# The down projection in seven block products, set between the tiles of gate and up, with weights handled in halves

## What is computed

```python
h2 = rms_norm(x, g_pre_ffn[l]) * (1.0 + sc2) + sh2
gate, up = jnp.split(h2 @ w_ffn_in[l], 2, axis=-1)      # 1024 x 2816 each
y = (jax.nn.silu(gate) * up) @ w_ffn_out[l]             # 2816 -> 1024
x = x + gt2 * rms_norm(y, g_post_ffn[l])
```

## Time and profile before

| | us |
|---|---|
| median of 3 runs | 1180.68 |
| range of the runs | 1180.19 to 1182.68 |
| span of the profiled execution | 1179.1 |
| PE busy in it | 1141.8 |
| DVE busy in it | 743.3 |
| POOL busy in it | 659.9 |
| ACT busy in it | 306.2 |

### The profile page before, as it was taken

The page is one execution under the profiler, slowest core; times in us unless marked ns, Lnnn a source line. Parts: engine busy times, 40 slices in busy tenths (PEclk is TensorE's granted clock), DMA queues, the critical chain, the costliest instruction groups (busy, mean ns, idle before and its releaser), DMA issues.

```text
span 1179.1 us, 13776 instructions
## 1 busy us (share of the span) xinstructions
PE 1141.8 (97%) x5528; PEld 952.8 (81%) x5528; DVE 743.3 (63%) x895; ACT 306.2 (26%) x460; POOL 659.9 (56%) x387
## 2 busy tenths in 40 slices
PE   2999999999999999999999999999999999999997
PEld 2788888888887888878888888888888888888885
DVE  6986979979997655658745454444444444444448
ACT  5645253362441624341110101010101010101014
POOL 4155343344342550325495958686867777777854
PEclk9999999999999999999999999999999999999999
DMA  9554323232211162211112121202020202020216
GB/s 329 175 161 123 108 74 106 73 107 75 87 36 37 39 231 88 89 36 54 36 36 72 36 72 36 72 26 83 20 88 18 89 19 90 19 89 18 89 32 272
DMA packets 94241, 98.52 MB, mean 84 GB/s; under 512 B 2941, under 2 KB 80994, under 8 KB 94178
## 3 DMA queue, kind: packets, MB, share of 16 engines
q1 hardware_dynamic: 92720, 93.33, 25.1%
q10 hardware_dynamic: 1458, 4.31, 0.9%
HBM read 89.25 MB, written 8.39 MB: 83 GB/s over the span
## 4 chain that ended last, share of the span: by engine, by line
PE 91%; DVE 4%; ACT 2%; issue 1%; SPq 1%; DMA 1%; DVEq 0%; ACTq 0%
PE pair L1732 30%; PE pair L1653 25%; PE pair L1545 24%; PE pair L1581 4%; PE pair L1710 1%; PE pair L1508 1%; DMA x<-in_x 1%; DVE sraw L1261 1%; DVE acc L963 1%; PE pair L1595 1%; PE pair L1576 1%; SPq L404 1%; PE pair L1469 1%; PE pair L1457 1%; PE pair L1597 1%
## 5 line engine op out<-in xcount | busy, mean ns | idle before, releaser
L1085 DVE SCALAR_TENSOR_TENSOR pair<-u,conv_w_col,pair 128x512 f32<-128x512 f32 x240 | 162.4, 748 | 1.2
L1397 DVE TENSOR_TENSOR yt<-yt,pair 128x1024 f32<-128x1024 f32 x80 | 97.5, 1219 | 95.0 <-PE pair L1653 95.0
L607 POOL TENSOR_TENSOR w_lo<-raw,w_hi 128x1024 fp32r<-128x1024 f32 x66 | 146.6, 2222 | 5.3
L605 POOL CAST w_hi<-raw 128x1024 fp32r<-128x1024 f32 x66 | 68.6, 1040 | 121.0 <-PE pair L1653 52.5
L528 POOL TENSOR_TENSOR w_lo<-raw,w_hi 128x1024 fp32r<-128x1024 f32 x21 | 52.4, 2500 | 103.3 <-ACT w_hi L693 103.3
L1653 PE MATMUL pair<-w_hi,u_hi 128*128 128x512 f32 x352 | 108.6, 390 | 0.3 <-DVE yt L1395 0.3
L1653 PE MATMUL pair<-w_hi,u_lo 128*128 128x512 f32 x352 | 108.4, 389 | 0.0
L1653 PE MATMUL pair<-w_lo,u_hi 128*128 128x512 f32 x352 | 108.4, 389 | 0.0
L607 POOL TENSOR_TENSOR w_lo<-sraw,w_hi 128x1024 fp32r<-128x1024 f32 x38 | 104.2, 2743 | 3.0
L605 POOL CAST w_hi<-sraw 128x1024 fp32r<-128x1024 f32 x38 | 39.5, 1039 | 117.8 <-PE pair L1653 116.0
L539 POOL TENSOR_TENSOR acc<-acc,ada 128x1024 f32<-128x1024 f32 x28 | 67.4, 2407 | 52.4 <-ACT ada L737 51.1
(11 more groups left out here) (260 smaller groups left out, 2584.0 us busy)
## 6 DMA issues: line engine op xcount, KB each, us to landing
ada<-in_w_ada SPq DMA_DIRECT2D x48, 512.0 KB, 3.9
raw<-in_w_ffn_in SPq DMA_DIRECT2D x44, 512.0 KB, 3.9
raw<-in_w_in SPq DMA_DIRECT2D x24, 512.0 KB, 3.8
raw<-in_w_ffn_out SPq DMA_DIRECT2D x22, 512.0 KB, 3.4
x<-in_x SPq DMA_DIRECT2D x8, 512.0 KB, 8.3
raw<-in_w_out SPq DMA_DIRECT2D x8, 512.0 KB, 3.4
x<-in_x SPq DMA_DIRECT2D x4, 1024.0 KB, 8.2
out<-x ACTq DMA_DIRECT2D x8, 512.0 KB, 2.6
```

The costliest lines, as they stand in the source:

```text
L605: me.done(pool.tensor_copy(w_hi[:, g % WS, cols], src[:, cols]))
L607: pool.tensor_tensor(w_lo[:, g % WS, cols], src[:, cols], w_hi[:, g % WS, cols], ALU.subtract).then_inc(w_split, 1)
L1085: i_ = dve.scalar_tensor_tensor(out=dst, in0=src, scalar=w, in1=dst, op0=ALU.mult, op1=ALU.add)
L1397: dve.tensor_tensor(yt[:, i, :], yt[:, i, :], pair[2 + n % 2][:, :], ALU.add).then_inc(y_added, 1)
```

## The change

Pairs of blocks are now (2 bk, 2 bk + 1). For bk = 0 to 9 the down projection of a pair is made of seven block products too: the tokens in two halves, the pair's two blocks of 128, and the output width in two halves. Each of the seven is 4 tiles of 128 tokens by 512 columns, 3 matmuls each (`down_tile`). The pair 10 stays plain (`end_tile`, 8 tiles of 12 matmuls). Gate and up are made of seven products from e = 2 on (`gu_product`).

PE's order becomes steps: one product of gate and up (12 matmuls, step `s` of block e), then two tiles of down (6 matmuls), so that the tiles of pair bk lie among the products of e = 2 bk + 2 and 2 bk + 3. A tile's bank (4 to 7) is read by DVE after each of the 28 tiles of a pair (`tile_sum`), and PE may write tile k when tile k - 4 has been read. Gate and up use banks 0 to 3 only; the second product that lands in a bank is accumulated onto the first, and silu is applied in the bank.

u is held in halves (`u1`, `u2a`, `u2b`). DVE makes four sums of them for each pair (`operand_sum`), ACT the high part (`operand_high`) and DVE the low part (`operand_low`) of each of seven operands. Weights are loaded in halves of 128 x 512 straight into the place where their low part will be made (256 KB each; four for each e, seven for each pair of down). Their sums are made by POOL (`gu_sums`, `down_sums`), their high parts by ACT (`gu_high_part`, `down_high_part`, two steps ahead), their low parts by POOL (`gu_low_part`, `down_low_part`). Their places are freed in order of the products, and SP's queue waits on the products and on the sums.

At the start of the block DVE's order is: one sum of token parts, u of e = 0, three differences, two low parts, one sum, one difference (all of 128 x 2048), u of e = 1 (`conv_product(1)`), one more low part, the operands of pair 0, and then the steps. Some of the full values that were summed again from parts are kept (`modulated_to`). At the end POOL combines the down results of pairs 0 to 9 (8 subtractions of 128 x 512 each), and `end_tile(0)` stands ahead of `gg_rows`.

The core of the diff (places, loads and the last pair's weights are left out):

```diff
+ITEMS = ["a0", "s2", "a1", "s1", "s3", "s4", "b1"]
+STEPS = len(ITEMS)
+LOADED = ["a0", "b0", "b1", "a1"]
+E0 = 2
+PAIRS = FB - 1
+N_STEPS = 2 * STEPS * PAIRS
+
+
+
+
+A11, S3, A22, A12, S1, S4, S2 = range(7)
+OPERAND = [A11, A12, S3, S4, S1, A22, S2]
+PRODUCT_OF = [OPERAND.index(n) for n in range(7)]
+TILES = 4
...
+            def weight_step(e, s):
+
+                m = step_at(e, s)
+                bk, n = divmod(m, 2 * STEPS)
+                if e + 1 < FFT:
+                    if s == 5:
+                        gu_sums(e + 1, "s2")
+                        gu_sums(e + 1, "s3")
+                    if s == 6:
+                        gu_sums(e + 1, "s4")
+                elif s in (2, 4, 5):
+                    for k in {2: (0,), 4: (1, 2), 5: (3,)}[s]:
+                        end_low_part(k)
+                gu_low_part(m + 2)
+                if e + 1 < FFT and s == 4:
+                    gu_sums(e + 1, "s1")
+                if n in (0, 2, 4, 6):
+                    down_sums(bk, n)
+                if n % 2 == 0:
+                    down_low_part(7 * bk + n // 2 + 1)
...
+                if m >= N_STEPS:
+                    return
+                e, s = E0 + m // STEPS, m % STEPS
+                k = ITEMS[s]
+                if k in gu_loaded:
+                    act.wait_ge(*of_loaded(k, e))
...
-                act.wait_ge(ufull_ready, e + 1)
-                if e >= 2:
-                    act.wait_ge(w_used, chunk_at("D", e // 2 * 2 - 1) + 1)
-                act.activation(u_hi[:, e % 2, :], ufull[:, :], ACT.Copy).then_inc(uhi_ready, 1)
-
...
+            def gate_step(e, s):
+
+                if s == 0:
+                    act.wait_ge(gu_done, step_at(e, 0) + 1)
+                    if e > E0:
+                        act.wait_ge(*of_sum(e - 1, 6))
+                    act.activation(p_sum, alpha(e), ACT.Copy).then_inc(gu_act, 1)
+                if s == 2:
+                    act.wait_ge(gu_done, step_at(e, 2) + 1)
+                    act.activation(alpha(e), alpha(e), ACT.Silu).then_inc(gu_act, 1)
+                if s == 5:
+                    act.wait_ge(*of_sum(e, 4))
+                    act.activation(gamma, gamma, ACT.Silu).then_inc(gu_act, 1)
+
+            def operands_behind(e, s):
+
+                bk = e // 2
+                if e % 2 == 0:
+                    if s == 0 and bk < PAIRS:
+                        operand_high(bk, S3, s3_raw, (op_sum, 4 * bk + 1))
+                    elif s == 0:
+                        operand_high(bk, S3, u2a, u2_ready(e))
+                    return
+                if s == 0:
+                    operand_high(bk, S1, u2a, (op_sum, 4 * bk + 2))
+                    operand_high(bk, S4, u1, (op_sum, 4 * bk + 4))
+                if s == 1:
+                    operand_high(bk, S2, s3_raw, (op_sum, 4 * bk + 3))
...
+            for e in range(E0, FFT):
+                for s in range(STEPS):
+                    m = step_at(e, s)
+                    gu_high_part(m + 2)
+                    if m % 2 == 0:
+                        down_high_part(m // 2 + 1)
+                    if e == FFT - 1 and s in (2, 4, 5):
+                        for k in {2: (0,), 4: (1, 2), 5: (3,)}[s]:
+                            end_high_part(k)
+                    operands_behind(e - 1, s)
+                    if (e, s) == (E0, 1):
+                        token_high(4, t_lo_f[:, 2, :, :], t_hi[:, 2, :, :])
+                    gate_step(e, s)
+                    if s == 6:
+                        if e % 2:
+                            operand_high(e // 2, A22, u2b, u2_ready(e))
+                        operand_high(e // 2, A12 if e % 2 else A11, u1, u1_ready(e))
...
+            def operand_sum(e, n):
+
+                bk = e // 2
+                if n == S3:
+                    dve.wait_ge(*u1_ready(e))
+                    if bk:
+                        dve.wait_ge(*operand_at(bk - 1, S2))
+                    i_ = dve.tensor_tensor(s3_raw[:, :], u1[:, :], u2a[:, :], ALU.subtract)
+                elif n == S1:
+                    dve.wait_ge(*u2_ready(e))
+                    dve.wait_ge(*operand_at(bk, S3))
+                    i_ = dve.tensor_tensor(u2a[:, :], u2a[:, :], u2b[:, :], ALU.add)
+                elif n == S2:
+                    i_ = dve.tensor_tensor(s3_raw[:, :], u2b[:, :], s3_raw[:, :], ALU.subtract)
                 else:
...
+                    dve.wait_ge(op_sum, 4 * bk + 3)
+                    dve.wait_ge(*operand_at(bk, A12))
+                    i_ = dve.tensor_tensor(u1[:, :], s3_raw[:, :], u1[:, :], ALU.subtract)
+                i_.then_inc(op_sum, 1)
...
+            def gu_step(e, s):
+
+                v = u2[e % 2][:, :]
+                if s in (1, 3, 4, 5, 6):
+                    dve.wait_ge(gu_done, step_at(e, s) + 1)
+                if s == 1:
+                    dve.wait_ge(*of_act(e, 1))
+                    gu_op(e, 1, p_sum, p_sum, beta(e), ALU.add)
+                if s == 3:
+                    dve.wait_ge(*of_sum(e, 1))
+                    if e % 2 == 0:
+                        dve.wait_ge(*operand_at(e // 2 - 1, S1))
+                    gu_op(e, 2, v, p_sum, gamma, ALU.add)
+                if s == 4:
+                    dve.wait_ge(*of_sum(e, 2))
+                    gu_op(e, 3, v, v, delta, ALU.add)
+                if s == 5:
+                    gu_op(e, 4, gamma, p_sum, gamma, ALU.add)
+                if s == 6:
+                    dve.wait_ge(*(operand_at(e // 2, S3) if e % 2 else operand_at(e // 2 - 1, S4)))
+                    gu_op(e, 6, u1[:, :], p_sum, delta, ALU.add)
+                    dve.wait_ge(*of_act(e, 2))
+                    dve.wait_ge(*of_sum(e, 6))
+                    gu_op(e, 7, u1[:, :], u1[:, :], alpha(e), ALU.mult)
+
+            def gated_second(e):
+
+                v = u2[e % 2][:, :]
+                dve.wait_ge(*of_act(e, 3))
+                gu_op(e, 5, v, v, gamma, ALU.mult)
+
+            def tile_sum(k):
+
+                d, t = divmod(k, TILES)
+                bk, q = divmod(d, 7)
+                made = {1: yt[:, t, 0:HALF], 3: yt[:, t, HALF:D], 5: yt[:, TILES + t, 0:HALF]}
+                dst = made[q] if q in made else yt[:, TILES + t, HALF:D]
+                dve.wait_ge(down_made, k + 1)
+                if bk == 0 and q in (0, 1, 3, 5):
+                    i_ = dve.tensor_copy(dst, bank(4 + t))
...
+            def operands_behind(e, s):
+
+                bk = e // 2
+                if e % 2 == 0:
+                    if s == 0:
+                        operand_low(bk, A11, u1)
+                        operand_low(bk, S3, s3_raw if bk < PAIRS else u2a)
                     return
...
+                if s == 0:
+                    if e > 1:
+                        operand_low(bk, A12, u1)
+                    else:
+                        operand_sum(e, S1)
+                        operand_sum(e, S2)
+                    operand_sum(e, S4)
+                if s == 1:
+                    operand_low(bk, S1, u2a)
+                if s == 2:
+                    operand_low(bk, S4, u1)
+
+            dve.wait_ge(h_ready, 32)
+            quarter_full(quarter_sum(3), 0, 0)
+            conv_product(0)
+            operand_low(0, A11, u1)
+            operand_sum(0, S3)
+            operand_low(0, S3, s3_raw)
+            me.wait()
+            difference(quarter_sum(3), quarter_sum(0), quarter_sum(3))
+            difference(quarter_sum(0), quarter_sum(1), quarter_sum(0))
+            dve.wait_ge(t_full, 1)
+            difference(quarter_sum(1), quarter_sum(1), quarter_sum(3))
+            dve.wait_ge(x1_stored, 16 * TT)
+            dve.wait_ge(turned, 32)
+            token_low(1, t_lo[:, 1, :, :], quarter_sum(0), t_hi[:, 1, :, :])
+            token_low(2, t_lo[:, 0, :, :], quarter_sum(1), t_hi[:, 0, :, :])
+            quarter_full(t_lo_f[:, 2, :, :], 1, 0)
+            me.wait()
+            dve.wait_ge(t_full, 3)
+            difference(t_lo_f[:, 2, :, :], t_lo_f[:, 2, :, :], quarter_sum(1))
+            conv_product(1)
+            token_low(3, quarter(h_lo, 0, 1), quarter_sum(3), quarter(h_hi, 0, 1))
+            operand_low(0, A22, u2b)
+            operand_low(0, A12, u1)
+            for e in range(E0, FFT):
+                for s in range(STEPS):
+                    m = step_at(e, s)
+                    if s == 6 and e % 2:
+                        if e < FFT - 1:
+                            operand_sum(e, S1)
+                            operand_sum(e, S2)
+                        operand_low(e // 2, A22, u2b)
+                    gu_step(e, s)
+                    if s == 6 and e % 2 == 0 and e // 2 < PAIRS:
+                        operand_sum(e, S3)
+                    operands_behind(e - 1, s)
+                    tile_sums(m)
+                    if s == 5:
+                        gated_second(e)
+                    if s == 2 and e % 2 == 0:
+                        operand_low(e // 2 - 1, S2, s3_raw)
```

(101 more changed lines are left out.)

631 lines of the change are left out of this document (336 added, 295 removed).

## The result

The changed kernel takes 1163.12 us (median of 4 runs, 1162.21 to 1163.81), against 1181.03 for the kernel before: ratio 0.9846, 95% interval 0.9832 to 0.9860. A second series gave 1161.99 and 0.9839 (0.9826 to 0.9853). The forecast was 1161.9, and 1160.3 for the profiled span, which came out at 1160.8.

What follows compares the result with a forecast made beforehand. PE's number of matmuls was taken as the bound: 1179.1 - 29.9 (matmuls) - 0.6 (old loss) + 9 (start) + 2.7 (junctions) = 1160.3 us span, 1161.9 as median. Range for 8 in 10: 1151 to 1174.

Steps and rivals of the forecast that it cites:

- main term: Down and gate/up on PE: 132 matmuls removed at 0.2267 us each, 29.9 us less, all on the path.
- Beside the path: Other engines and loads within a pair's 57.1 us: DVE 43.2 us, POOL 42.6, ACT 21.4; queues priced at 0.
- the price c: Time of one DVE operation with both inputs in SBUF, 128x512: between 0.68 and 1.97 us, taken as 1.3.
- The junctions: Between pairs, end of odd e: PE may wait for ACT's copy; 0.3 us at nine places, 2.7 us, bounds 0 and 30.
- 5.7 + 5c from T(13): Time from step 13's start to ACT's copy of product 0, c per DVE SBUF operation; PE needs it at 12.2 us.
- The start: Start of the block, where the main loss was expected: PE waits costing 9 us net, bounds 1 and 13.
- the first wait: Start of the block: PE waits 4.7 us at the first down tile for DVE's product of e = 1.
- the second wait: Start of the block: PE waits 5.4 us at product 2 of e = 2 for ACT's copy.
- the short durations: DVE's times alone at the start, 2.28 us wide and 0.68 small: no first wait, 0.8 us at product 2.
- The slower clock behind a long wait: Matmuls behind each long PE wait might run slower: at most 1.3 us per wait, taken as 0.
- rival C: Junctions between pairs late by about 1.2 us each (c near 1.55): 1170 us; chance 22%.
- The end: Tail keeps its form, 8.8 us behind the last matmuls; POOL's eight subtractions cost 0, bounds 0 and 2.

Runs made afterwards that it cites:

- two_of_three: Changed kernel with the third matmul of each seven-product down tile (low part of u by high weights) left out, 280 fewer; 1107.85 us, ratio 0.9379.
- high_on_pool: Changed kernel with the high parts of all weights moved back from ACT to POOL; 1191.76 us, ratio 1.009 to the kernel before.
- POOL filled: Changed kernel with POOL making weight sum S4 three times instead of once at each junction, same result, to fill its idle gap; 1167.95 us, ratio 0.9884.
- low_first: Changed kernel with POOL making the first two low parts of weights before its sum S4; 1162.99 us, ratio 0.9849.
- copy_first: Changed kernel with ACT copying product 0 before it makes the operands' high parts; 1160.74 us, ratio 0.9830.
- after_again: The changed kernel itself, unedited, timed and profiled again as the measure for the other runs; 1161.99 us, ratio 0.9839.
- swap_places: Changed kernel with weights S1 and S4 exchanging places, so S1's low part lies in ring_m_r instead of S4's; 1162.63 us (one run).
- start_order: Changed kernel with ACT's copy and POOL's low parts moved earlier, and DVE's last wide difference and wide low part moved into steps 1 and 4; 1160.19 us, ratio 0.9825.

## Why the prediction was right, point by point

**The bound and the main term: right, and shown.** 132 x 0.2267 = 29.9 us is all that is gained; the other terms take some of it back. 4.08 us a step is what most steps took, across changes of bank and of stationary tile, so the price 0 for these was right. `two_of_three` shows that a matmul more or less still counts for eight to nine tenths of its distance.

**Beside the path: right.** SP's queue, the loads and ACT never appear among PE's waits in a pair. The means behind it, groups on DVE and POOL in the kernel after, 600 to 1120 us (xcount | busy, mean ns | idle):

```profile
L1665 DVE TENSOR_TENSOR yt<-yt,pair 128x512 f32<-128x512 f32 x251 | 167.5, 684 | 31.9 <-PE pair L2097 31.9
L1585 DVE TENSOR_TENSOR op_lo<-u2a,op_hi 128x512 fp32r<-128x512 f32 x10 | 15.5, 1548 | 0.0
...
L1585 DVE TENSOR_TENSOR op_lo<-s_raw,op_hi 128x512 fp32r<-128x512 f32 x17 | 13.0, 764 | 0.0
```

```profile
L760 POOL TENSOR_TENSOR raw_r<-raw,w_hi 128x512 fp32r<-128x512 f32 x61 | 85.3, 1399 | 61.0 <-ACT w_hi L1112 61.0
```

DVE's operations with one input in PSUM took 0.684, as read the earlier trace rows; those with both in SBUF 0.68 to 1.6 in the means of their groups, about 1.0 over all of them. DVE was busy 37.8 us of a pair, where 43.2 was said: the price c of 1.3 was too high. POOL's 43.97 answers to 42.6. The bound of "too much on POOL" was only reasoned; `high_on_pool` shows that moving the high parts to ACT was a condition of the gain: without it all of the gain and 11 us more are lost.

**The junctions: the term was 2.7 us, and what came was no wait at all.** The formula, 5.7 + 5c from T(13), holds up well. With the measured five operations, 5.07 us in all, it gives 10.8, and the copy stood 10.2 behind T(13) (665.35 to 675.53). With POOL filled it gives 5.7 + 7.34 = 13.0, where 12.2 is in time; PE waited 0.2 us. What failed is the value of c: the mean of the five was 1.01. The prediction itself had the reason at hand (POOL waits for ACT in that stretch) and took a mean of the old order all the same. The Trainium skill's rule in "SBUF — State Buffer", section "Who interferes with whom", says of a VectorE operation with two SBUF inputs and a GpSimd operation that reads SBUF that the later one waits for the whole of the earlier. The rows agree that they hold each other up: the same operation took 0.68 in POOL's gap and 1.78 with POOL at work. What decides is where POOL's gaps lie, not that it is busy for three quarters of a pair.

**The start: 9 forecast, 10.5 measured; the anchor was right, the first wait and the clock were not.** (1) The first wait was put at the first down tile, 4.7 us on DVE's product of e = 1. It came one product earlier, 2.65 us, on POOL's low part, for which the prediction had "0 to 2" and took nothing by itself. The cause is the meeting of the two engines, read from the other side. DVE and POOL in the kernel after:

```profile
542.28 3.37 DVE L1609 TENSOR_TENSOR t_lo_f<-hb_hi,hb_lo 128x2048 f32<-128x2048 f32 x1
545.68 3.24 DVE L1613 TENSOR_TENSOR t_lo_f<-t_lo_f,yt 128x2048 f32<-128x2048 f32 x1
```

```profile
540.17 3.33 POOL L750 TENSOR_TENSOR ring_m<-raw,w_lo_f 128x512 f32<-128x512 f32 x1
543.46 3.31 POOL L760 TENSOR_TENSOR raw_r<-raw,w_hi 128x512 fp32r<-128x512 f32 x1
546.74 3.33 POOL L769 TENSOR_TENSOR w_lo<-w_lo_f,w_hi 128x512 fp32r<-128x512 f32 x1
```

A POOL operation of 1.3 us took 3.3 beside DVE's wide ones, time after time (543.46, then 546.74, while DVE's begin at 542.28 and 545.68): the two take turns. 2.65 us lies above the bound of 2. The prediction counted the price of meeting on DVE's side alone. `low_first` shows that DVE's chain stood right behind: with POOL's wait gone, the wait at the down tile appears, 3.2 us, and nothing is gained. (2) The second wait, 5.4 forecast on ACT's copy, was 4.2 (step 1 took 4.4 more than 4.08), and `copy_first` shows its cause. Product 2 was forecast at 563.2 and began at 561.15. Of these 2.05 us, 0.65 is the earlier begin of `gate_up(1)` in this execution; most of the rest is DVE's seven wide operations, 21.0 us in all (527.95 to 548.92) where 22.05 stood. From the end of `gate_up(1)` to product 2 the start thus lost 8.8 us, where the sum had 10.1 and took 1 off: this chain, DVE's work to the copy, is what the prediction had right. With the short durations the prediction says 0.8 for the second wait; its own anchors give 0.2 (546.2 + 2.28 + 5 x 0.68 + 1.3 = 553.2 against 553.0), which changes nothing in the forecast. (3) The slower clock behind a long wait was bounded at 1.3 us each and taken at 0, since the old block's short gaps showed none of it. It cost 1.8 and 1.7, above the bound. Only the second counts: `after_again` and `swap_places` have the first wait without a slower stretch behind it and come to the same 89.56 and 89.55 us to step 14, since PE then waits for DVE and POOL instead. The 1.7 us behind product 2 is what makes 10.5 of 8.8. The wait that `low_first` uncovers is followed by slow matmuls too.

**How near the number came is partly luck.** Against the forecast of 1160.3 for the span stand four errors: -2.7 (no junction waits), +1.5 (the start), +2.4 (the distance of the matmuls) and -0.7 (earlier phases). They add up to 0.5. The main term and the path are not luck; an error of half a microsecond is.

**The prediction's own signs.** Of its signs of being right, the 936 matmuls of the down part and the wait at product 2 came. The wait at the first down tile did not come in the changed kernel, not all matmuls are 0.2267 us apart, and DVE was busy 37.8 us in a pair and not 43. Of its signs of being wrong, one came: a wait on a weight's low part, since POOL's operations at the start were priced as if they met nobody. The others (no wait at the start, pairs over 58 us, a longer tail) did not.

**The distance of the matmuls.** 2.4 us in the ten pairs come with two places of the weights (shown for `ring_m_r`, argued for `ggb_r`). The prediction had such a rise only as 1% under rival C, with more waits per matmul as its reason; here it was 0.4%. That it fills up the junctions' 2.7 us is chance.

**The end: right.** From the last matmuls to the end of the span (rows 15: 8.7 us), and POOL's eight subtractions, in the kernel after:

```profile
1151.49 0.61 PE L2120 MATMUL pair<-w_lo,op_lo 128*128 128x512 f32 x2
```

```profile
1124.51 10.95 POOL L847 TENSOR_TENSOR yt<-yt 128x512 f32<-128x512 f32 x8 [2.18 <-DVE yt L1665]
1138.58 2.41 POOL L853 TENSOR_TENSOR x<-x,xs 128x1024 f32<-128x1024 f32 x1 [3.12 <-DVE xs L1551]
```

1160.8 - 1152.10 = 8.7. POOL's first residual waits 3.12 us for DVE, so the subtractions hold nothing up.

## What to carry to other kernels

Where one engine's instructions fill the span, count them and price them by their distance; then spend the remaining effort on the places where the cover is thinnest, the start of a phase and the seams between its periods. When VectorE and GpSimd both work from SBUF, cost the meeting for both of them, and place by place: whether the other has a gap just there decides more than its share of busy time. A wait that is removed shows the next one behind it, so before moving one operation forward, follow what stands second on each engine.

## What the runs showed of the hardware

- Behind PE's waits of 2.5 and 4.2 us in the kernel after, the granted clock was 0.62 over the next 4.5 us and the matmuls were 0.43 us apart (its lower level, 1.2 GHz) for six to eight of them: 1.7 to 1.8 us each time. Ahead of the waits it was 1.00. A wait has no fixed price: in `after_again` and `swap_places` the same wait of 2.5 us was followed by matmuls 0.23 us apart, and so were the waits of 1.0 and 1.2 us in `copy_first`. What decides it stays open.
- With the low part of the stationary weights in `ring_m_r`, matmuls were 0.23 to 0.24 us apart instead of 0.2267, and the distance moved with the place. The cause stays open.
- DVE's 128 x 2048 operations (2.28 alone, rows 10) and POOL's 128 x 512 (1.29, rows 6) took 3.3 us each while they alternated: 1.0 us more for the one and 2.0 for the other, each a little less than the other's whole time. Beside the two wide operations that `start_order` moved, POOL alone paid: it took 3.44 and 3.35 us, and they took 2.27 and 2.30.
